# gMLP norm from batch-norm statistics, and a first norm by token halves

## The chip, the cores and the metric

The kernel runs on one core of a Trainium2 chip. The metric is the device time of the whole program in microseconds (us). TensorE is called PE, VectorE DVE, ScalarE ACT, GpSimd POOL and SyncE SP.

## The reference

256 tokens of width 1024 pass through two blocks of two layers each, all in fp32. The first block is, per layer, an RMS norm, a mixer (convolution and pooling in the even layer "ev", attention in the odd layer "od") and a gated feed-forward net. The second block has a latent-attention layer and a gMLP layer, each followed by a squared-ReLU net. What the change touches is the very first norm and the gMLP:

```python
def rmsnorm(x, g):
    y = xf * lax.rsqrt(jnp.mean(xf * xf, axis=-1, keepdims=True) + RMS_EPS)
    return (y * g).astype(x.dtype)

def even_mixer(h, w_in, conv_w, pool_w, pool_scale, w_out):
    z = h @ w_in                                  # 1024 -> 2048
    ...

def gmlp_mixer(h, w_in, ln_g, ln_b, ws, bs, w_out):
    z = jax.nn.gelu(h @ w_in, approximate=False)  # 1024 -> 4096
    u, v = z[..., :GM_HALF], z[..., GM_HALF:]     # GM_HALF = 2048
    v = layernorm(v, ln_g, ln_b)                  # mean and variance over 2048
    vc = v.reshape(B, S // GM_CHUNK, GM_CHUNK, GM_GROUPS, GM_GROUP_DIM)
    mixed = jnp.einsum('gpq,bnqgc->bnpgc', ws, vc) + bs.T[None, None, :, :, None]
    return (u * mixed.reshape(B, S, GM_HALF)) @ w_out
```

## The kernel before

**Weights.** All weights stream through four slots `raw` of 128 x 2048 numbers, loaded by SP in the order of use (`load(t)` for tile t, T_EV = 0 being the first). Every tile is split in two: ACT copies it to `w_hi` in PE's rounded fp32 (L508), DVE subtracts to get `w_lo` (L984), and each product is three matmuls (hi x hi, lo x hi, hi x lo). A slot of `raw` is loaded anew once DVE has split it (`lo_done`); `w_hi` and `w_lo` are written anew once PE has used the tile (`w_used`). `split(t)` is written into ACT's and DVE's programs by hand, and each engine works through its own program in order, so the place of a split among the other work decides when it runs.

**A norm.** Tokens lie on partitions, in two halves of 128 (`t` = 0, 1; the residual `h` is 128 x 2 x 1024). ACT squares and sums, POOL forms rstd, DVE scales (`hs`), PE transposes to features on partitions, ACT applies the gain (L533) and DVE makes `xn_hi` and `xn_lo` (`take`, L1010 and L1012). In most stages this goes by token halves (`norm` on ACT, `boundary` on DVE). The stage then begins with `head` on PE (L1717): the first two weight tiles are multiplied for token half 0 while half 1 is still in the norm (its transposes stand inside), then for half 1. The results have tokens on partitions; ACT copies them (`head_copy`, L574) and PE transposes them in the middle of the third tile (`head_out`, L1741).

**The first stage before.** x comes in one transfer, ahead of the first weight tile; then come sixteen transfers of small rows (gains, biases, convolution weights; L464) that PE transposes into `vec` (L1774), then the other weight tiles. The first norm runs over whole rows: `squares`, `scale`, `norm`, `gains`, `take`, in pieces of both halves. PE then does all eight input tiles with `f_tile` (L1609), 48 matmuls of 256 columns each, in banks 0 to 3, the first from L1622. The mixer's pooling and convolution on ACT and DVE run beside it. The pool matmuls are at L1791.

**gMLP.** PE first forms v in four column pieces c of 512, for both halves (`t_half`), two weight tiles a piece. ACT applies Gelu into `gm_v` with a sum beside it (L884). After the last piece DVE forms the mean (L1512, L1513), ACT squares the eight pieces less the mean (L894), DVE sums (L1516), POOL makes rstd (`root`, L2212 and L2214). DVE normalizes piece q with two operations for each half (`gm_norm`, L1528 and L1535) and copies a slice of 256 columns for PE (`gm_slice`, L1548). Meanwhile PE forms two tiles of u (`gm_u(0)`, `gm_u(1)`), and then mixes (`gm_mix`, L2159). A DVE step (`gm_step`, from L1554) adds the bias, multiplies by u and makes `a_lo` (L1566) for the output product; after the eighth step PE's `t_tail` (L1684) ends the stage. T_GM is the first u tile; T_GM + 2 and T_GM + 3 are the tiles that PE takes after the first mixing.

Of the kernel before, what the change touches and what calls it, by code (L numbers as in the profile page):

```python
# [23 lines left out]
ALU = mybir.AluOpType  # L24
# [3 lines left out]
P = 128  # L28
# [63 lines left out]
def build(nc, I, out):  # L92
    ctx = ExitStack()
    with ctx:
# [196 lines left out]
        in_h, in_cst, in_rows, in_small = sem("in_h"), sem("in_cst"), sem("in_rows"), sem("in_small")  # L291
# [46 lines left out]
        WHOLE = ("ev", "ctx")  # L338
# [159 lines left out]
        def _(act):  # L498
# [13 lines left out]
            def squares(name, src):  # L512

                for t in range(TT):
                    if name == "ctx":
                        act.wait_ge(ctx_in, 16)
                    else:
                        act.wait_ge(in_h, 16)
# [17 lines left out]
            def gains(name, gain, shift=None):  # L536
# [4 lines left out]
                if name == "ev":  # L541
                    act.wait_ge(vec_ready, 1)
# [1864 lines left out]
```

## Time and profile before

| | |
|---|---|
| median of three runs | 1346.9 us (1343.85 to 1347.37) |
| the profiled execution's own time | 1346.17 us |
| its span | 1344.4 us |
| PE busy | 1295.0 us, 96% |
| DVE busy | 940.4 us, 70% |
| ACT busy | 651.6 us, 48% |
| POOL busy | 117.0 us, 9% |
| DMA | 265.32 MB, mean 197 GB/s |
| mean granted PE clock | 0.983 |

The span is the profiled stretch on the core; the time around it is 1.8 us more. Busy shares are of the span. A matmul's duration in the trace runs to its modelled end, so matmuls that follow each other every 0.12 us are shown as 0.28 us each. Times in the rows are us from the span's start.

### The profile page before, as it was taken

How to read it: one execution, taken by the hardware profiler on the slowest of the kernel's cores; microseconds unless marked ns; L12 is line 12 of the kernel's file. 1: busy time of each engine (PE TensorE's matmuls, PEld its weight loads, DVE VectorE, ACT ScalarE, POOL GpSimd, SP SyncE). 2: the span in 40 equal slices, each digit the busy share in tenths (PEclk: the TensorE clock that was granted, in tenths of full speed). 3: DMA queues.
4: the chain of work that ended last, by engine and by line, in shares of the span. 5: the costliest groups of instructions: out<-in, count | busy, mean ns of one | idle time of the engine just before them, and what ended most of it. 6: DMA issues, size and time to landing. Idle time of an engine off the chain costs nothing.

```text
span 1344.4 us, 20759 instructions
## 1 busy us (share of the span) xinstructions
PE 1295.0 (96%) x8261; PEld 1155.8 (86%) x8261; DVE 940.4 (70%) x1168; ACT 651.6 (48%) x981; POOL 117.0 (9%) x226
## 2 busy tenths in 40 slices
PE   6999999999999999999789989999999899999998
PEld 5989999999777999999667768999888789889997
DVE  4867888856574688897455646998765589676654
ACT  4565444554353654454545635544445443554441
POOL 2000000000100021111012210111010000000000
PEclk9999999999998999999889999999999899999999
DMA  9636777745621498893222242999546378377540
GB/s 298 234 127 222 249 249 240 230 126 182 200 75 54 135 325 312 309 336 103 67 65 94 65 155 94 338 391 378 189 144 233 125 252 311 126 250 234 187 156 32
DMA packets 155660, 265.32 MB, mean 197 GB/s; under 512 B 5756, under 2 KB 116219, under 8 KB 155590
## 3 DMA queue, kind: packets, MB, share of 16 engines
q1 hardware_dynamic: 139094, 204.94, 45.6%
q0 software_dynamic: 16352, 58.98, 12.4%
q8 instruction: 49, 0.80, 0.2%
q10 hardware_dynamic: 144, 0.43, 0.1%
q14 instruction: 21, 0.17, 0.0%
HBM read 263.26 MB, written 1.06 MB: 197 GB/s over the span
## 4 chain that ended last, share of the span: by engine, by line
PE 85%; DVE 8%; ACT 3%; issue 2%; POOL 1%; DMA 0%; POOLq 0%; ACTq 0%; DVEq 0%
PE ps L1641 24%; PE ps L1622 12%; PE ps L1623 12%; PE ps L1624 12%; DVE w_lo L984 2%; PE ps L1684 2%; PE ps L1686 2%; PE ps L1685 2%; PE ps L1662 1%; PE ps L1664 1%; PE ps L1663 1%; PE ps L1733 1%; PE ps L1734 1%; PE ps L1735 1%; PE ps L2024 1%
## 5 line engine op out<-in xcount | busy, mean ns | idle before, releaser
L984 DVE TENSOR_TENSOR w_lo<-raw,w_hi 128x2048 fp32r<-128x2048 f32 (+3 forms) x215 | 442.7, 2071 | 137.9 <-ACT w_hi L508 137.6
L508 ACT ACTIVATE w_hi<-raw 128x2048 fp32r<-128x2048 f32 (+3 forms) x215 | 373.3, 1741 | 159.2 <-PE ps L1641 115.5
L1622 PE MATMUL ps<-xn_hi,w_hi 128*128 128x256 f32 x1440 | 411.3, 286 | 2.8 <-DVE xn_lo L1012 2.8
L1623 PE MATMUL ps<-xn_lo,w_hi 128*128 128x256 f32 x1440 | 409.5, 284 | 0.0
L1624 PE MATMUL ps<-xn_hi,w_lo 128*128 128x256 f32 x1440 | 409.3, 284 | 0.0
L1622 PEld LDWEIGHTS ps<-xn_hi,w_hi 128*128 128x128 f32 x1440 | 278.3, 193 | 5.6 <-issue 3.6
L1623 PEld LDWEIGHTS ps<-xn_lo,w_hi 128*128 128x128 f32 x1440 | 278.2, 193 | 2.2 <-issue 0.5
L1624 PEld LDWEIGHTS ps<-xn_hi,w_lo 128*128 128x128 f32 x1440 | 278.1, 193 | 0.0
L1641 PE MATMUL ps<-w_hi,a_hi 128*128 128x512 f32 x464 | 145.7, 395 | 0.9 <-DVE a_lo L1241 0.9
L1641 PE MATMUL ps<-w_lo,a_hi 128*128 128x512 f32 x464 | 144.1, 392 | 0.0
L1641 PE MATMUL ps<-w_hi,a_lo 128*128 128x512 f32 x464 | 143.6, 391 | 0.0
L1063 DVE SCALAR_TENSOR_TENSOR acc<-side,cs,acc 128x1024 f32<-128x1024 f32 x84 | 104.0, 1279 | 0.2
L1641 PEld LDWEIGHTS ps<-w_lo,a_hi 128*128 128x128 f32 x464 | 87.7, 189 | 19.0
L1641 PEld LDWEIGHTS ps<-w_hi,a_lo 128*128 128x128 f32 x464 | 87.4, 188 | 18.9
L1641 PEld LDWEIGHTS ps<-w_hi,a_hi 128*128 128x128 f32 x464 | 84.0, 190 | 16.5 <-DVE a_lo L1241 1.2
L2248 POOL DMA_DIRECT2D side<-in_ada_w x76 | 41.2, 542 | 355.6 <-DVE acc L1063 262.8
L853 ACT ACTIVATE work<-ps 128x512 f32<-128x512 f32 x32 | 19.1, 596 | 106.9 <-PE ps L1624 100.6
L647 ACT ACTIVATE work<-ps,vec 128x256 f32<-128x256 f32 x44 | 22.4, 560 | 85.8 <-PE ps L1624 79.4
L1178 DVE SCALAR_TENSOR_TENSOR work<-ps,vec,work 128x255 f32<-128x255 f32 (+1 forms) x88 | 38.3, 477 | 23.2 <-ACT work L647 21.0
L1684 PE MATMUL ps<-w_hi,a_hi 128*128 128x512 f32 x128 | 50.8, 397 | 0.7 <-DVE a_lo L1566 0.7
L1686 PE MATMUL ps<-w_hi,a_lo 128*128 128x512 f32 x128 | 49.9, 390 | 0.0
L1685 PE MATMUL ps<-w_lo,a_hi 128*128 128x512 f32 x128 | 49.9, 389 | 0.0
(293 smaller groups left out, 1795.4 us busy)
## 6 DMA issues: line engine op xcount, KB each, us to landing
raw<-in_ffn_w SPq DMA_DIRECT2D x64, 1024.0 KB, 5.6
side<-in_ada_w POOLq DMA_DIRECT2D x96, 512.0 KB, 6.4
raw<-in_ffn_w_in SPq DMA_DIRECT2D x44, 1024.0 KB, 5.4
raw<-in_ffn_w_out SPq DMA_DIRECT2D x32, 512.0 KB, 5.6
raw<-in_gm_w_in SPq DMA_DIRECT2D x16, 1024.0 KB, 5.8
raw<-in_od_w_in SPq DMA_DIRECT2D x12, 1024.0 KB, 5.5
raw<-in_ev_w_in SPq DMA_DIRECT2D x8, 1024.0 KB, 12.7
raw<-in_gm_w_out SPq DMA_DIRECT2D x8, 1024.0 KB, 5.6
```

The lines of the kernel that those rows point to most:

```text
L508: nc.scalar.activation(w_hi[s][:, 0:w], raw[s][:, 0:w], ACT.Copy).then_inc(hi_done, 1)
L984: nc.vector.tensor_tensor(w_lo[s][:, 0:w], raw[s][:, 0:w], w_hi[s][:, 0:w].bitcast(F32), ALU.subtract)\
L1063: nc.vector.scalar_tensor_tensor(acc[:, slot, :], tile, cs[:, bass.ds(val(kb), 1)], acc[:, slot, :], ALU.mult, ALU.add).then_inc(side_used, 1)
L1178: nc.vector.scalar_tensor_tensor(av, ps[bank][:, b * S:b * S + S - shift], vcol("ffn_conv_w", j * 2 + (n * 3 * FFB + tap * FFB + b)), av, ...
L1622: nc.tensor.matmul(o, hi, xn_hi3[:, k, :], start=k == 0, stop=False)
L1623: nc.tensor.matmul(o, hi, xn_lo3[:, k, :], start=False, stop=False)
L1624: last = nc.tensor.matmul(o, lo, xn_hi3[:, k, :], start=False, stop=k == KB - 1)
L1641: ins = nc.tensor.matmul(o, x_part, w, start=begin and x_part is xh and w_part == 0, stop=end and x_part is xl)
L1684: nc.tensor.matmul(o, xh, hi, start=first and i == 0 and m == 0, stop=False)
L1685: nc.tensor.matmul(o, xh, lo, start=False, stop=False)
L1686: last = nc.tensor.matmul(o, xl, hi, start=False, stop=i == 1 and m == len(blocks) - 1)
L2248: pool.dma_start(side[:, s.c % SLOTS, :], ada_view(layer, comp0 + m % n_comp, kb))\
```

## The change

**gMLP.** The Gelus give no sums any more. DVE takes batch-norm statistics (`bn_stats`, six numbers) of each piece of 512 for each half right behind its Gelu, and two `bn_aggr` merge the four sets of a half to mean and variance. POOL adds EPS to the variance and takes the power. ACT's eight squares and DVE's reductions are gone; ACT splits tiles T_GM + 2 and T_GM + 3 right behind the last Gelus. On DVE the splits of the two tiles stand behind the first norm and slice.

**The first stage.** x comes in two transfers with a semaphore each: half 0 first, then the sixteen small rows, then the first weight tile, then half 1, then the other tiles. The first norm goes by halves, and the stage uses `head`, `head_copy` and `head_out`. The banks of the six remaining tiles move by two.

```diff
@@ SP
-            sp.dma_start(h[:, :, :], I["x"][0].rearrange("(t p) d -> p t d", p=P)).then_inc(in_h, 16)
+            x_v = I["x"][0].rearrange("(t p) d -> p t d", p=P)
+            sp.dma_start(h[:, 0, :], x_v[:, 0, :]).then_inc(in_h[0], 16)
...
-            load(T_EV)
-
             at = 0
             stage = wk(6144, ROW_TILES * P).rearrange("p (r c) -> p r c", r=ROW_TILES)
             for name, n in ROWS:
...
+            load(T_EV)
+            sp.dma_start(h[:, 1, :], x_v[:, 1, :]).then_inc(in_h[1], 16)
             for t in range(T_EV + 1, T_FFN0):
                 load(t)
@@ ACT
-            squares("ev", h)
+            half_squares("ev", 0)
             split(T_EV)
-            gains("ev", lambda b: col("mix_norm_g", b))
+            half_gains("ev", 0, ev_gain)
+            half_squares("ev", 1)
             split(T_EV + 1)
+            half_gains("ev", 1, ev_gain)
+            head_copy("ev", T_EV)
             split(T_EV + 2)
             split(T_EV + 3)
...
+            act.wait_ge(head_ps, HEAD["ev"] + 1)
             for m in range(2):
-                act.wait_ge(w_used, T_EV + m + 1)
...
-                    nc.scalar.activation(gm_v[:, t, 512 * c:512 * c + 512], ps[GM_BANK[c] + t][:, :], ACT.Gelu,
-                                         accum_out=st[:, 48 + 4 * t + c:49 + 4 * t + c]).then_inc(GM["v"], 1)
-                if c < 3:
-                    split(T_GMV + 2 * c + 4)
-                    split(T_GMV + 2 * c + 5)
-            for t in range(TT):
-                act.wait_ge(GM["mu"], 1)
-                for c in range(4):
-
-                    junk = ps[4 + c][:, :] if t else acc[:, 3 + c // 2, 512 * (c % 2):512 * (c % 2) + 512]
-                    nc.scalar.activation(junk, gm_v[:, t, 512 * c:512 * c + 512], ACT.Square,
-                                         bias=st[:, 58 + t:59 + t], accum_out=st[:, 64 + 4 * t + c:65 + 4 * t + c])\
-                        .then_inc(GM["sq"], 1)
-            split(T_GM + 2)
-            split(T_GM + 3)
+                    nc.scalar.activation(gm_v[:, t, 512 * c:512 * c + 512], ps[GM_BANK[c] + t][:, :], ACT.Gelu).then_inc(GM["v"], 1)
+                split(T_GMV + 2 * c + 4)
+                split(T_GMV + 2 * c + 5)
@@ DVE
-            dve.wait_ge(in_h, 16)
-            scale("ev", h)
-            split(T_EV)
-
             dve.wait_ge(vec_ps, 1)
             nc.vector.tensor_copy(vec[:, 0:N_ROWS], ps[4][:, 0:N_ROWS]).then_inc(vec_ready, 1)
-            take("ev")
+            dve.wait_ge(in_h[0], 16)
+            half_scale("ev", 0)
+            split(T_EV)
+            take("ev", 0)
+            dve.wait_ge(in_h[1], 16)
+            half_scale("ev", 1)
...
             split(T_EV + 1)
+            take("ev", 1)
             split(T_EV + 2)
             split(T_EV + 3)
...
+            def gm_stats(c):
+                for t in range(TT):
+                    dve.wait_ge(GM["v"], 2 * c + t + 1)
+                    at = 40 + 24 * t + 6 * c
+                    nc.vector.bn_stats(st[:, at:at + 6], gm_v[:, t, 512 * c:512 * c + 512]).then_inc(GM["sq"], 1)
+
+            gm_stats(0)
...
+            for c in range(1, 3):
+                gm_stats(c)
+                split(T_GMV + 2 * c + 4)
+                split(T_GMV + 2 * c + 5)
+            gm_stats(3)
             dve.wait_ge(GM["sq"], 8)
-            nc.vector.tensor_reduce(st[:, 60:62], st[:, 64:72].rearrange("p (t c) -> p t c", t=TT), AX.X, ALU.add)\
-                .then_inc(GM["norm"], 1)
+            for t in range(TT):
+                nc.vector.bn_aggr(st[:, 4 + 2 * t:6 + 2 * t], st[:, 40 + 24 * t:64 + 24 * t]).then_inc(GM["norm"], 1)
...
-            split(T_GM + 2)
             gm_norm(0)
-            split(T_GM + 3)
...
             gm_slice(0)
+            split(T_GM + 2)
+            split(T_GM + 3)
@@ PE
             pe.wait_ge(in_cst, 16)
-            norm("ev")
...
             last.then_inc(vec_ps, 1)
+            transposes("ev", 0)
...
-            for m in range(8):
+            head("ev", T_EV)
+            for m in range(2, 8):
                 if m in free:
                     pe.wait_ge(*free[m])
-                f_tile(T_EV + m, m % 4, fresh="ev" if m == 0 else None)
+                else:
+                    pe.wait_ge(head_cp, 2 * HEAD["ev"] + m - 1)
+                f_tile(T_EV + m, (m - 2) % 4, mid=(lambda: head_out("ev")) if m == 2 else None)
@@ POOL
-            pool.wait_ge(GM["norm"], 1)
-            root(36, 2, [(60, 2, GMH)]).then_inc(GM["rstd"], 1)
+            pool.wait_ge(GM["norm"], 2)
+            for t in range(TT):
+                chain(nc.gpsimd.tensor_scalar(rs[:, 36 + t:37 + t], st[:, 5 + 2 * t:6 + 2 * t], 1.0, EPS, ALU.mult, ALU.add))
+            nc.gpsimd.tensor_tensor(rstd[:, 36:38], rs[:, 36:38], half[:, 0:2], ALU.pow).then_inc(GM["rstd"], 1)
```

The order of the work moves in two places. ACT at the start, before (L521 squares, L508 splits, L533 gains, L602 the first copy out of the input product):

```order
L521 ACTIVATE work,st<-h 128x1024 x2
L508 ACTIVATE w_hi<-raw 128x2048
L533 ACTIVATE work<-ps,vec 128x256 x8
L508 ACTIVATE w_hi<-raw 128x2048 x3
L590 ACT_TABLE_LOAD
```

and in the changed kernel (its own line numbers: L530 squares, L510 splits, L535 gains, L581 and L583 the two head copies), from half 1's squares on, with what each waits for (the same for half 0 and the first tile stands ahead of it):

```order
L530 ACTIVATE work,st<-h 128x512 [waits in_h1] x2
L510 ACTIVATE w_hi<-raw 128x2048 [waits raw_full1]
L535 ACTIVATE work<-ps,vec 128x128 [waits xt_ps,vec_ready]
L535 ACTIVATE work<-ps,vec 128x128 x3
L535 ACTIVATE work<-ps,vec 128x128 [waits xt_ps]
L535 ACTIVATE work<-ps,vec 128x128 x3
L581 ACTIVATE work<-ps 128x512 [waits head_t]
L583 ACTIVATE work<-ps 128x512 [waits w_used]
L510 ACTIVATE w_hi<-raw 128x2048 [waits raw_full2]
L510 ACTIVATE w_hi<-raw 128x2048 [waits raw_full3]
```

The splits of the third and fourth tile now stand behind the two head copies, the second of which waits until two tiles are used.

DVE around the gMLP norm, before (L984 splits, L1512 to L1516 sums, L1528 and L1535 the norm, L1548 the slice, L1554 the first step):

```order
L984 TENSOR_TENSOR w_lo<-raw,w_hi 128x2048 x4
L1512 TENSOR_REDUCE st<-st 128x2
L1513 TENSOR_SCALAR st<-st 128x2
L1516 TENSOR_REDUCE st<-st 128x2
L984 TENSOR_TENSOR w_lo<-raw,w_hi 128x2048
L1528 SCALAR_TENSOR_TENSOR work<-work,st,side 128x512 x2
L1535 SCALAR_TENSOR_TENSOR work<-work,rstd,side 128x512 x2
L984 TENSOR_TENSOR w_lo<-raw,w_hi 128x2048
L1548 COPY acc<-work 128x512
L1554 TENSOR_TENSOR acc<-ps,work 128x512
```

and in the changed kernel (L980 splits, L1534 and L1541 the norm, L1552 the slice, L1558 the first step):

```order
L1507 BN_STATS st<-work 128x6 x2
L980 TENSOR_TENSOR w_lo<-raw,w_hi 128x2048 x2
L1507 BN_STATS st<-work 128x6 x2
L1522 BN_AGGR st<-st 128x2 x2
L1534 SCALAR_TENSOR_TENSOR work<-work,st,side 128x512 x2
L1541 SCALAR_TENSOR_TENSOR work<-work,rstd,side 128x512 x2
L1552 COPY acc<-work 128x512
L980 TENSOR_TENSOR w_lo<-raw,w_hi 128x2048 x2
L1558 TENSOR_TENSOR acc<-ps,work 128x512
```

Both splits have moved behind the first slice, and the statistics stand behind each Gelu pair, ahead of the splits.

## Rows read from the trace of the kernel before

**Rows 1.** Who waited for whom, PE (total us, times, longest).

```profile
PE ps L2159 <- DVE acc L1548: 5.7, 1, 5.7
```

**Rows 2.** Timeline of PE's first real matmul; line L1791's matmuls (min/median/max ns).

```profile
17.46 0.35 PE L1622 MATMUL ps<-xn_hi,w_hi 128*128 128x256 f32 x1 [2.79 <-DVE xn_lo L1012]
...
L1791 PE MATMUL ps<-a_hi,w_hi x4: 283/283/283, 65.4 to 66.5; 128*128 128x256 f32 x4
```

**Rows 3.** Timeline of SP's issues: start us, us, what, [idle before].

```profile
1.88 1.99 SPq L464 DMA_DIRECT2D work<-in_mix_norm_g  x1
3.92 0.53 SPq L464 DMA_DIRECT2D work<-in_ffn_norm_g  x1
...
8.88 0.25 SPq L464 DMA_DIRECT2D work<-in_mla_k_norm  x1
...
9.53 25.90 SPq L409 DMA_DIRECT2D raw<-in_ev_w_in  x7
```

**Rows 4.** Timeline of ACT at the start.

```profile
10.36 1.91 ACT L508 ACTIVATE w_hi<-raw 128x2048 fp32r<-128x2048 f32 x1 [0.96 <-DMA raw<-in_ev_w_in]
15.29 3.03 ACT L533 ACTIVATE work<-ps,vec 128x256 f32<-128x256 f32 x8 [3.01 <-DVE vec L1103]
```

**Rows 5.** Timeline of ACT in gMLP, from the last Gelu to the tile splits.

```profile
1049.48 0.59 ACT L884 ACTIVATE work<-ps 128x512 f32<-128x512 f32 x1
...
1056.25 3.70 ACT L508 ACTIVATE w_hi<-raw 128x2048 fp32r<-128x2048 f32 x2
```

**Rows 6.** Timeline of POOL in gMLP.

```profile
1056.70 0.19 POOL L2212 TENSOR_SCALAR rs<-st 128x2 f32<-128x2 f32 x1 [43.77 <-DVE st L1516]
1056.97 0.72 POOL L2214 TENSOR_TENSOR rstd<-rs,half 128x2 f32<-128x2 f32 x1
```

**Rows 7.** Timeline of DVE in gMLP, from the mean to the first step.

```profile
1050.19 0.16 DVE L1512 TENSOR_REDUCE st<-st 128x2 f32<-128x8 f32 x1 [4.58 <-ACT work L884]
...
1058.25 2.29 DVE L984 TENSOR_TENSOR w_lo<-raw,w_hi 128x2048 fp32r<-128x2048 f32 x1 [1.64 <-ACT w_hi L508]
1060.46 1.41 DVE L1528 SCALAR_TENSOR_TENSOR work<-work,st,side 128x512 f32<-128x512 f32 x2
...
1065.56 0.42 DVE L1548 COPY acc<-work 128x512 f32<-128x512 f32 x1
1068.21 0.69 DVE L1554 TENSOR_TENSOR acc<-ps,work 128x512 f32<-128x512 f32 x1 [2.24 <-PE ps L2159]
```

**Rows 8.** Timeline of PE in gMLP: last of u, first and last mixing, tail.

```profile
1066.03 2.08 PE L2159 MATMUL ps<-work,acc 128*128 128x128 f32 x8 [5.67 <-DVE acc L1548]
...
1136.06 1.06 PE L2159 MATMUL ps<-work,acc 128*128 128x128 f32 x8
...
1144.63 0.47 PE L1684 MATMUL ps<-w_hi,a_hi 128*128 128x512 f32 x1 [0.66 <-DVE a_lo L1566]
```

**Rows 9.** Timelines of ACT (copy) and DVE (half norm) in the first stages.

```profile
34.14 0.58 ACT L602 ACTIVATE work<-ps 128x512 f32<-128x512 f32 x1
34.62 1.91 ACT L508 ACTIVATE w_hi<-raw 128x2048 fp32r<-128x2048 f32 x1
...
87.01 0.88 DVE L1000 TENSOR_SCALAR work<-h,rstd 128x512 f32<-128x512 f32 x2 [1.78 <-POOL rstd L2227]
...
89.72 0.29 DVE L1010 CAST xn_hi<-work 128x256 fp32r<-128x256 f32 x1 [1.23 <-ACT work L533]
...
90.39 0.28 DVE L1010 CAST xn_hi<-work 128x256 fp32r<-128x256 f32 x1
```

**Rows 10.** Page, DMA issues (KB, median us to landing); line L409's landing, window 9.5:10.

```profile
raw<-in_ev_w_out SPq DMA_DIRECT2D x4, 1024.0 KB, 5.0
...
DMA to landing us min/median/max: 5.9/5.9/5.9
```

**Rows 11.** PE by stretches: us, busy (x), granted clock, DMA share, GB/s.

```profile
18.40:21.85 3.45, 3.42 (x17) 0.53 0.78 183
1066.00:1069.80 3.80, 3.77 (x17) 0.50 0.82 233
```

More of the change, by code:

```diff
@@ L290, in build @@
         side_used = sem("side_used")
-        in_h, in_cst, in_rows, in_small = sem("in_h"), sem("in_cst"), sem("in_rows"), sem("in_small")
+        in_h = [sem(f"in_h{t}") for t in range(TT)]
+        in_cst, in_rows, in_small = sem("in_cst"), sem("in_rows"), sem("in_small")
         vec_ps, vec_ready, cs_ready = sem("vec_ps"), sem("vec_ready"), sem("cs_ready")
@@ L336, in build @@
         RCOL = dict({n: 2 * k for n, k in NORM.items()}, final=18)
-        WHOLE = ("ev", "ctx")
+        WHOLE = ("ctx",)
         def counts(names, whole, halves):
@@ L350, in build @@
         XN = counts(NORM, 4, 8)
-        HEAD = {n: k for k, n in enumerate(["ffn0", "od", "ffn1", "relu0", "relu1"])}
-        TB = {"ffn0": (2, 3), "od": (2, 3), "ffn1": (2, 3), "lat": (2, 4), "relu0": (4, 5), "gm": (2, 3), "relu1": (2, 3)}
+        HEAD = {n: k for k, n in enumerate(["ev", "ffn0", "od", "ffn1", "relu0", "relu1"])}
+        TB = {"ev": (2, 3), "ffn0": (2, 3), "od": (2, 3), "ffn1": (2, 3), "lat": (2, 4), "relu0": (4, 5), "gm": (2, 3), "relu1": (2, 3)}
         def u_at(j, base):
@@ L514, in squares @@
                 for t in range(TT):
[L515 to L518, printed above, removed]
+                    act.wait_ge(ctx_in, 16)
                     c = RCOL[name] + t
-                    junk = wk(4096 + D * t, D) if name == "ctx" else hs[:, t, :]
+                    junk = wk(4096 + D * t, D)
                     nc.scalar.activation(junk, src[:, t, :], ACT.Square, accum_out=st[:, c:c + 1]).then_inc(sq_done, 1)
@@ L526, in half_squares @@
                 for c in range(2):
-                    act.wait_ge(h_ready, h_count(name, t, c))
+                    if name == "ev":
+                        act.wait_ge(in_h[t], 16)
+                    else:
+                        act.wait_ge(h_ready, h_count(name, t, c))
                     nc.scalar.activation(hs[:, t, 512 * c:512 * c + 512], h[:, t, 512 * c:512 * c + 512], ACT.Square,
@@ L554, in half_gains @@
                     act.wait_ge(mod_ready, MOD_COUNT[name])
+                if name == "ev":
+                    act.wait_ge(vec_ready, 1)
                 for i in range(4):
@@ L597, in _ @@
             ev_u = wk(2564, 4 * 272).rearrange("p (g t) -> p g t", g=4)
+            act.wait_ge(head_ps, HEAD["ev"] + 1)
             for m in range(2):
-                act.wait_ge(w_used, T_EV + m + 1)
                 if m == 0:
                     act.wait_ge(EV["pin"], 1)
-                nc.scalar.activation(ev_u[:, 2 * m:2 * m + 2, 16:272], ps[m][:, :].rearrange("p (g t) -> p g t", g=2), ACT.Copy)\
+                nc.scalar.activation(ev_u[:, 2 * m:2 * m + 2, 16:272], ps[2 + m][:, :].rearrange("p (g t) -> p g t", g=2), ACT.Copy)\
                     .then_inc(EV["pool"], 1)
@@ L607, in _ @@
                 act.wait_ge(w_used, t + 1)
-                nc.scalar.activation(ev_c, ps[(2 + 3 * m) % 4][:, :], ACT.Copy).then_inc(EV["gate"], 1)
+                nc.scalar.activation(ev_c, ps[3 * m % 4][:, :], ACT.Copy).then_inc(EV["gate"], 1)
                 split(t + 4)
@@ L1160, in _ @@
             dve.wait_ge(rows_ps, 1)
-            nc.vector.tensor_copy(bias_rows, ps[2][0:8, 0:511]).then_inc(rows_sb, 1)
+            nc.vector.tensor_copy(bias_rows, ps[0][0:8, 0:511]).then_inc(rows_sb, 1)
             for j in range(2):
@@ L1507, in _ @@
                 nc.vector.tensor_copy(gm_wst[:, 512 * c:512 * c + 512], ps[6 + c][:, :]).then_inc(GM["ws"], 1)
-            for j in range(2, 6):
-                split(T_GMV + j + 4)
-            dve.wait_ge(GM["v"], 8)
-            chain(nc.vector.tensor_reduce(st[:, 56:58], st[:, 48:56].rearrange("p (t c) -> p t c", t=TT), AX.X, ALU.add))
-            nc.vector.tensor_scalar(st[:, 58:60], st[:, 56:58], -1.0 / GMH, None, ALU.mult).then_inc(GM["mu"], 1)
-            dve.wait_ge(GM["mu"], 1)
+            for c in range(1, 3):
[3 more added lines that the diff above has]
+            gm_stats(3)
             dve.wait_ge(GM["sq"], 8)
-            nc.vector.tensor_reduce(st[:, 60:62], st[:, 64:72].rearrange("p (t c) -> p t c", t=TT), AX.X, ALU.add)\
-                .then_inc(GM["norm"], 1)
+            for t in range(TT):
+                nc.vector.bn_aggr(st[:, 4 + 2 * t:6 + 2 * t], st[:, 40 + 24 * t:64 + 24 * t]).then_inc(GM["norm"], 1)
+            dve.wait_ge(GM["norm"], 2)
             dve.wait_ge(GM["rstd"], 1)
@@ L1527, in gm_norm @@
                 for t in range(TT):
-                    last = nc.vector.scalar_tensor_tensor(vv[t], vv[t], st[:, 58 + t:59 + t], gain, ALU.add, ALU.mult)
+                    last = nc.vector.scalar_tensor_tensor(vv[t], vv[t], st[:, 4 + 2 * t:5 + 2 * t], gain, ALU.subtract, ALU.mult)
                 if q % 2:
@@ L1788, in _ @@
             for g in range(4):
-                o = ps[g // 2][:, (g % 2) * S:(g % 2) * S + S]
+                o = ps[2 + g // 2][:, (g % 2) * S:(g % 2) * S + S]
                 hi, lo = parts(T_POOL % SLOTS, g * P, P)
@@ L1802, in _ @@
                     pe.wait_ge(rb_ready, 16)
-                    nc.tensor.matmul(ps[2][0:8, 0:511], rel[:, :], onehot, start=True, stop=True).then_inc(rows_ps, 1)
+                    nc.tensor.matmul(ps[0][0:8, 0:511], rel[:, :], onehot, start=True, stop=True).then_inc(rows_ps, 1)
             def ev_ready(i):
```

11 lines of the change are left out of this document (6 added, 5 removed).

## The prediction

> **What bounds the kernel now.** I first read who waited for whom on TensorE (PE). PE is busy for 96% of the span, so an edit counts only where PE stands still or where PE gets more to do. Two of its waits lie where the change works: 5.7 us for the first slice of the gMLP norm (L1548) [rows 1], and the start, where the first real matmul waits for `xn_lo` (L1012). From 17.46 us to the pool matmuls at 65.4 us PE doesn't stop again [rows 2].
>
> The start: the SP queue issues all of x and the first weight tile, then sixteen row transfers from 1.88 us, and the other tiles from 9.53 us [rows 3]. The first tile can be split by ScalarE (ACT) at 10.36 us, and the eight gain copies run from 15.29 us [rows 4].
>
> The gMLP norm: between the last Gelu and the first mixing matmul there is a chain. ACT ends the Gelu at 1050.1 us, squares eight pieces, and only then splits the next two weight tiles, from 1056.25 us [rows 5]. GpSimd gives rstd at 1057.7 us [rows 6]. VectorE (DVE) waits for the tile split, not for rstd: split (2.29), norm from 1060.46 us, a second split, slice at 1065.56 us [rows 7]. PE ends its second u tile at 1060.4 us and mixes at 1066.03 us, at half clock [rows 8].
>
> **Part 1, the gMLP norm.** The eight squares, their eight reads, two reductions and the eight reads behind the Gelus go; eight bn_stats and two bn_aggr come on DVE. Six bn_stats stand in stretches where DVE waits for ACT (4.58 us idle before L1512 [rows 7]; the same kind of gap is there behind each Gelu pair), so they cost nothing; only the last pair is on the chain. No row shows a bn_stats. From below it is half of the 0.88 us of two tensor-scalars over 512 [rows 9], 0.44 us; from above two passes at 1.41/2 = 0.7 us each [rows 7], 1.4 us. I take one such pass, 0.7 us, as the row that reads as many fp32 numbers once. An aggregate over 24 numbers I put at 0.2 us.
>
> The new chain: the last Gelu ends at 1050.1; its bn_stats 0.7, two aggregates 0.4; GpSimd now two small operations (0.27 from start to start, by 1056.70 and 1056.97 [rows 6]) and the power 0.72, so 1.3; hand-overs 0.2. DVE starts its norm at 1052.7. Norm 2.9 (the 5.1 from 1060.46 to the slice at 1065.56, less 2.2 for the split that now goes behind), slice 0.4: done at 1056.0, 4.4 us before PE is through with the u tiles. So PE's wait of 5.7 us goes wholly. The two splits (4.5 us) follow, DVE is free at 1060.5. ACT makes its halves of them from 1050.1 to 1053.8, in the place of the squares.
>
> What is late next: the mixing matmuls start at 1060.4, and at full clock eight take 1.06 us instead of 2.08 [rows 8]. DVE's first step therefore starts at 1061.4, not at 1068.21 [rows 7]: **6.8 us** earlier. From that step on DVE is the tighter engine: its steps follow each other with only the 0.7 and 1.1 us for ACT's half between them, down to the last `a_lo`, for which PE waits at 1144.63 [rows 8]. So what PE wins beyond 6.8 us, by running its next u tile at full clock as well, it loses there, where its wait grows from 0.66 to some 1.5 us. Gain: 6.8 us; if bn_stats costs 1.4 us, DVE is free at 1062.0 and the gain is 6.2.
>
> **Part 2, the start.** The first weight tile now stands behind x's first half and the sixteen row transfers. The fifteen later rows are issued from 3.92 to 9.53 us [rows 3]; the first took 1.99 us with 2 MB in flight ahead of it, which I put at 0.5 when only half of x is. The rows start at 1.4 (the 1.88 of before less the weight tile's own issue), so the weight tile is issued at 1.4 + 0.5 + 5.6 = 7.5, and a little less if the others speed up too: I take 7.3. Bounds: 7.0 and 9.5. A 1 MB tile takes 5.0 us to landing on a quiet queue and took 5.9 at 9.53 us [rows 10]; I take 5.2. It lands at **L = 12.5**, against 10.36 at the latest before. The Trainium skill, DMA: Bandwidth & Descriptors, section Anatomy of one DMA, gives 2.0 us plus the bytes at 436 GB/s, an estimate of 4.4 us for 1 MB: by it L would be 11.7 and the sum 0.8 us smaller. By that formula the trace does not agree: 5.0 and 5.9 us [rows 10].
>
> From L on, each with its row [rows 4, 7, 9, 11]: ACT half 1.9, DVE half 2.3, first cast and rest 0.7, hand-overs 0.3. The first matmul starts at L + 5.2 = 17.7, so hardly later than now (17.46): the landing is later by 2 us, but gains and rows are no longer behind it. Then:
> - Second tile: DVE first takes half 0 (four times 0.67), scales half 1 (0.9) and splits (2.3): ready at L + 10.3 = 22.8. The 24 matmuls on the first tile's first half are done at 20.6, or 22.8 at half clock. PE goes on at 22.9.
> - 24 matmuls at 0.12 us (384 of them fill 17.46 to 65.4 us less 1.7 for the clock [rows 2, 11]), 2.9; half 1's eight transposes, now inside, 0.9; token half 1's 48 matmuls 5.8, 0.2 for their first operand: the head ends at L + 20.1 = 32.6.
> - **The new wait.** ACT's queue now has the two head copies ahead of the split of the third tile, and the second copy waits until both tiles are used up. In the norms further on, both splits stand ahead of the copies. So PE finishes the head and then stands still for a copy (0.5 until ACT's next start [rows 9]), the ACT half 1.9, the DVE half 2.3, hand-overs 0.2: **4.9 us**. The third tile starts at 37.5.
> - Six tiles at 5.76 us, 34.6, and the eight head transposes, 0.9. After the 2.79 us of idling at the start PE ran 3.4 us at a granted clock of 0.53, and after 5.67 us of idling in gMLP 3.8 us at 0.50 (1.2 of 2.4 GHz) [rows 11]: half of each stretch, 1.6 and 1.9 us, was lost. I take 1.7 here.
>
> The pool matmuls start at 74.6 instead of 65.4: **+9.2 us**. What follows is the old order with its banks renamed, and PE-bound; the side loads of GpSimd go out some 6 us later, are wanted only in the first feed-forward stage, and cost nothing. The second half of x lands right behind the first tile, before its squares are due. Bounds: a rows pace of before without any relief and a landing of 5.9 us make L 15.4 and the term 12.1, rows issued by 7.0 and 5.0 us to landing (L = 12.0) and a clock that costs 0.7 make it 7.7.
>
> **Sum.** +9.2 - 6.8 = +2.4 us. The profiled execution took 1346.17 us (span 1344.4), 0.7 under the median of 1346.9, so the sum gives 1348.6 on its own scale and 1349.3 on the median's. A measurement of this kernel tells some 0.3%, 4.0 us, from no change; +2.4 is within.
>
> **The rivals.**
> - *The start costs more, slower by over 0.3%.* Mechanism: the row transfers keep their pace of before and hold the first weight tile back in SP's queue; each us of L is a us of the end. It decides from L = 14.1 on (+10.8 - 6.8). For it: one row still took 0.25 us to issue late in the series [rows 3]; against it: the 1.99 us of the first one went with 2 MB in flight. At L = 15.4: +5.3, 1352.2. A clock that stays low for twice as long (+1.7) does the same from L = 12.4. Chance 0.28.
> - *The wait behind the head is hidden.* If PE were held at the third tile less than I think, for example because the clock stays up, the term is 7.7 and the sum +0.9 or, with PE's whole gain in gMLP (7.6, if DVE weren't the tighter one), +0.1: 1347.0 to 1347.8, still no difference. Inside my 0.64.
> - *Faster by over 0.3%.* The change of order would have to cost under 2.8 us. It does if the third tile's split is not on the path, which the order of ACT's queue speaks against: without the 4.9 us and the 1.7 of clock the sum is -4.2, 1342.7. Chance 0.08.
> - *bn_stats is dear, over 3 us a piece.* Then the last pair pushes the norm out by 4.8 us, DVE is free at 1065.3, and the gain falls to 2.9: 1353.2. Every one-pass row over 512 numbers says no; 0.03, within the slower case.
>
> **How the numbers follow.** Within 0.3%: 0.64, my forecast, +2.4 us with its own range of -1 to +4. Slower 0.28, faster 0.08. The range must leave out 2 in 10: 1345.8 takes in the small start term (+0.9) and 2 us for a median of three runs that spread over 3.5 us; 1353.0 takes in the late landing of the first tile.
>
> **What would show each step.** The first real matmul near 17.7 us, PE's second wait near 22 us, a third wait of 4.9 us ahead of the third tile with ACT's queue on a copy, a low granted clock behind it, the pool matmuls near 74.6 us. In gMLP no wait at the first mixing matmul and no low clock there; bn_stats near 0.7 us; the distance from the last Gelu to the last `a_lo` shorter by 6.8 us; PE's wait before it near 1.5 us. I am wrong if the third tile starts right behind the head, if the first tile lands after 14 us, or if another stage moves.

## The result, and the profile after

Over 17 runs of each on the same chip, the kernel before took 1346.05 us (1338.64 to 1347.37) and the changed one 1349.95 us (1345.95 to 1353.39). The ratio is 1.0029, with a 95% interval of 1.0017 to 1.0042: 3.9 us slower, the size of what a measurement of this kernel can just tell from nothing. The forecast was 1349.3 us, 2.4 us slower.

| | before | after |
|---|---|---|
| profiled execution's own time | 1346.17 us | 1353.39 us |
| its span | 1344.4 us | 1351.7 us |
| PE busy | 1295.0 us | 1300.1 us |
| DVE busy | 940.4 us | 946.5 us |
| ACT busy | 651.6 us | 647.3 us |
| mean granted PE clock | 0.983 | 0.982 |

The profiled execution is the longest of the 17, so part of its 7.3 us of extra span has to be found in something that other executions don't show.

I read first who waited for whom on PE. The columns are, as in [rows 1], total us, times and longest:

```profile
PE ps L1778 <- DMA work<-in_ada_b: 8.8, 1, 8.8
PE ps L1739 <- DVE xn_lo L1008: 6.3, 3, 5.8
...
PE ps L1628 <- DVE w_lo L980: 4.9, 1, 4.9
...
PE ps L1690 <- DVE a_lo L1570: 1.1, 1, 1.1
```

The wait of 5.7 us for the first slice [rows 1] is gone, and a new one of 4.9 us stands there, for the split of a weight tile. The last row is the end of gMLP, where PE waited 0.66 us before [rows 8]. PE's timeline at the start, those rows that begin after idling, shows where:

```profile
18.44 0.55 PE L1739 MATMUL ps<-w_hi,xn_hi 128*128 128x256 f32 x1 [5.77 <-DVE xn_lo L1008]
38.60 0.55 PE L1628 MATMUL ps<-xn_hi,w_hi 128*128 128x256 f32 x1 [4.90 <-DVE w_lo L980]
```

The first real matmul is 1 us later than in [rows 2]. There is no wait ahead of the second tile in this trace: PE went through the first tile's matmuls at half pace until 23.70 us, and the second tile's split was done at 23.3. The third tile starts at 38.60 us, and the pool matmuls, last row below, 11.2 us later than in [rows 2]:

```profile
L1799 PE MATMUL ps<-a_hi,w_hi x4: 283/283/283, 76.6 to 77.7; 128*128 128x256 f32 x4
```

The timeline of SP (against [rows 3]) shows how the first tile comes to be late:

```profile
1.31 0.41 SPq L464 DMA_DIRECT2D work<-in_mix_norm_g  x1
1.78 0.41 SPq L464 DMA_DIRECT2D work<-in_ffn_norm_g  x1
...
7.36 0.43 SPq L411 DMA_DIRECT2D raw<-in_ev_w_in  x1
```

The first row now goes out in 0.41 us instead of 1.99, the others take as long as before, and the tile is issued at 7.36 us. The answer for this one issue gives its landing:

```profile
DMA to landing us min/median/max: 6.0/6.0/6.0
```

ACT's timeline (against [rows 4]) shows both the late tile and the order of the queue:

```profile
13.39 1.91 ACT L510 ACTIVATE w_hi<-raw 128x2048 fp32r<-128x2048 f32 x1 [6.28 <-DMA raw<-in_ev_w_in]
...
28.23 0.65 ACT L581 ACTIVATE work<-ps 128x512 f32<-128x512 f32 x1
33.74 0.60 ACT L583 ACTIVATE work<-ps 128x512 f32<-128x512 f32 x1 [4.86 <-PE ps L1741]
34.23 3.70 ACT L510 ACTIVATE w_hi<-raw 128x2048 fp32r<-128x2048 f32 x2
```

From 28.88 to 33.74 us ACT stands at the second head copy until PE has used both tiles; the splits of the third and fourth tile are queued behind it. PE, through with the head, then waits for the copy, ACT's half (1.9) and DVE's half of the third tile. That is the wait of 4.90 us. What it costs afterwards is in PE's stretches (us, PE, PEld, DVE, ACT and POOL busy with counts, granted clock, DMA share, GB/s):

```profile
38.40:44.20 5.80, 5.60 (x26) 5.63 (x27) 2.26 (x2) 1.05 (x2) 0.00 (x0) 0.50 0.79 252
...
790.10:809.40 19.30, 17.37 (x49) 10.47 (x49) 5.64 (x9) 2.43 (x6) 0.00 (x0) 0.73 0.22 76
```

Behind the wait PE runs at half clock (1.2 of 2.4 GHz) until 44.2 us: of 5.6 us, 2.8 are lost. The second row is a stretch some 750 us later, in a stage that the change doesn't edit. It ran at a mean granted clock of 0.73 and took 19.3 us; the execution profiled of before has the same 49 matmuls at full clock in 14.6 us:

```profile
780.70:795.30 14.60, 12.61 (x49) 8.04 (x50) 5.64 (x9) 2.44 (x7) 0.00 (x0) 1.00 0.30 101
```

gMLP after, DVE's timeline (against [rows 7]):

```profile
1063.66 1.29 DVE L1507 BATCH_NORM_STATS2 st<-work 128x6 f32<-128x512 f32 x2 [4.10 <-ACT work L892]
1064.98 0.39 DVE L1522 BATCH_NORM_AGGREGATE st<-st 128x2 f32<-128x24 f32 x2
1066.82 1.42 DVE L1534 SCALAR_TENSOR_TENSOR work<-work,st,side 128x512 f32<-128x512 f32 x2 [1.44 <-issue]
...
1069.72 0.43 DVE L1552 COPY acc<-work 128x512 f32<-128x512 f32 x1
1070.06 4.49 DVE L980 TENSOR_TENSOR w_lo<-raw,w_hi 128x2048 fp32r<-128x2048 f32 x2
1075.51 0.69 DVE L1558 TENSOR_TENSOR acc<-ps,work 128x512 f32<-128x512 f32 x1 [0.96 <-PE ps L2167]
```

The statistics of two pieces take 1.29 us and the two aggregates 0.39. The slice is done at 1070.15 us, and PE, which needs it next, takes it without a wait and at full clock, and so against [rows 8] in 1.06 us, not 2.08:

```profile
1074.35 1.06 PE L2167 MATMUL ps<-work,acc 128*128 128x128 f32 x8
```

**Where the 7.3 us of span are.** I took DVE's 215 tile splits of both traces in pairs and read how far each starts behind its counterpart, which gives the lag at every point of the program. It is +11.0 us once the first stage is under way, 14.15 us ahead of the gMLP norm, and +7.3 us from the first split behind it to the end. So: start +11.2 us, gMLP -6.85 us, and +2.95 us from other places: +4.8 us in the stretch at a clock of 0.73, less what other stretches gave back. Is that stretch the change's doing? Read from 775 to 812 us, the traces of this case show a granted clock of 0.86 here, of 0.95 in two more kernels with the new first stage, and of 1.00 in the other two with it and in all four with the old one, though PE idles for the same 1.88 us there in all nine. With one execution of each kernel that does not tell chance from an effect of the later start; it stays open. The medians, over 17 runs each, are 3.9 us apart, about what the start's and gMLP's parts come to without that stretch.

### The profile page after: what moved, and what is told of

The parts are those of the page before. It is cut to its first block, busy times and chain, and to the rows that moved or that the text cites. A ratio compares the mean times of both kernels' runs of the same rounds, so it can differ in the third digit from the quotient of the medians.

```text
span 1351.7 us, 20790 instructions
## 1 busy us (share of the span) xinstructions
PE 1300.1 (96%) x8269; PEld 1158.7 (86%) x8269; DVE 946.5 (70%) x1185; ACT 647.3 (48%) x971; POOL 117.3 (9%) x229
## 3 DMA queue, kind: packets, MB, share of 16 engines
HBM read 263.26 MB, written 1.06 MB: 196 GB/s over the span
## 4 chain that ended last, share of the span: by engine, by line
PE 86%; DVE 8%; ACT 3%; issue 2%; POOL 1%; DMA 0%; SPq 0%; POOLq 0%; ACTq 0%; DVEq 0%
PE ps L1647 24%; PE ps L1628 12%; PE ps L1630 12%; PE ps L1629 12%; DVE w_lo L980 2%; PE ps L1739 2%; PE ps L1690 2%; PE ps L1692 2%; PE ps L1691 2%; PE ps L1668 1%; PE ps L1741 1%; PE ps L1740 1%; PE ps L1669 1%; PE ps L1670 1%; PE ps L2032 1%
## 5 line engine op out<-in xcount | busy, mean ns | idle before, releaser
L980 DVE TENSOR_TENSOR w_lo<-raw,w_hi 128x2048 fp32r<-128x2048 f32 (+3 forms) x215 | 442.7, 2072 | 132.7 <-ACT w_hi L510 132.4
L510 ACT ACTIVATE w_hi<-raw 128x2048 fp32r<-128x2048 f32 (+3 forms) x215 | 373.1, 1741 | 155.5 <-PE ps L1647 116.0
L1628 PE MATMUL ps<-xn_hi,w_hi 128*128 128x256 f32 x1408 | 402.5, 286 | 4.9 <-DVE w_lo L980 4.9
L1630 PE MATMUL ps<-xn_hi,w_lo 128*128 128x256 f32 x1408 | 400.7, 285 | 0.0
L1629 PE MATMUL ps<-xn_lo,w_hi 128*128 128x256 f32 x1408 | 400.7, 285 | 0.0
L1628 PEld LDWEIGHTS ps<-xn_hi,w_hi 128*128 128x128 f32 x1408 | 272.5, 194 | 7.3 <-issue 5.6
L1647 PE MATMUL ps<-w_hi,a_hi 128*128 128x512 f32 x464 | 146.7, 398 | 1.1 <-DVE a_lo L1239 0.9
L1647 PE MATMUL ps<-w_lo,a_hi 128*128 128x512 f32 x464 | 144.8, 393 | 0.0
L1647 PE MATMUL ps<-w_hi,a_lo 128*128 128x512 f32 x464 | 144.4, 392 | 0.0
L1739 PE MATMUL ps<-w_hi,xn_hi 128*128 128x256 f32 x192 | 56.9, 296 | 6.4 <-DVE xn_lo L1008 6.3
L1740 PE MATMUL ps<-w_lo,xn_hi 128*128 128x256 f32 x192 | 55.3, 288 | 0.0
L1741 PE MATMUL ps<-w_hi,xn_lo 128*128 128x256 f32 x192 | 55.3, 288 | 0.0
```

The lines of the kernel that those rows point to most:

```text
L510: nc.scalar.activation(w_hi[s][:, 0:w], raw[s][:, 0:w], ACT.Copy).then_inc(hi_done, 1)
L980: nc.vector.tensor_tensor(w_lo[s][:, 0:w], raw[s][:, 0:w], w_hi[s][:, 0:w].bitcast(F32), ALU.subtract)\
L1628: nc.tensor.matmul(o, hi, xn_hi3[:, k, :], start=k == 0, stop=False)
L1629: nc.tensor.matmul(o, hi, xn_lo3[:, k, :], start=False, stop=False)
L1630: last = nc.tensor.matmul(o, lo, xn_hi3[:, k, :], start=False, stop=k == KB - 1)
L1647: ins = nc.tensor.matmul(o, x_part, w, start=begin and x_part is xh and w_part == 0, stop=end and x_part is xl)
```

## The experiments

Each kernel ran in five rounds beside the kernel before; ratios are against it, with 95% intervals. Four ran on one chip (before: 1344.29 us, 26 runs), the last three on another (1344.58 us, 27 runs). The first two kernels run the two halves of the sum apart, the next two ask what the start loses by, two more what in gMLP gives the gain, and the last repairs the start.

### gMLP's part alone

The kernel before, with only the gMLP part of the change:

```diff
-                    nc.scalar.activation(gm_v[:, t, 512 * c:512 * c + 512], ps[GM_BANK[c] + t][:, :], ACT.Gelu,
-                                         accum_out=st[:, 48 + 4 * t + c:49 + 4 * t + c]).then_inc(GM["v"], 1)
+                    nc.scalar.activation(gm_v[:, t, 512 * c:512 * c + 512], ps[GM_BANK[c] + t][:, :], ACT.Gelu).then_inc(GM["v"], 1)
...
+            gm_stats(3)
...
-            split(T_GM + 2)
             gm_norm(0)
-            split(T_GM + 3)
...
             gm_slice(0)
+            split(T_GM + 2)
+            split(T_GM + 3)
```

> The kernel before with the gMLP part of the change alone. My theory: the two parts add up, so this one gives -6.8 us (ratio 0.995), all of it between the last Gelu and DVE's first gMLP step; the first stage is as before. Rival: the gMLP part gains nothing by itself, because DVE's work behind it is as tight as before (ratio 1.000).

Measured: 1337.17 us (1331.73 to 1340.04, 9 runs), ratio 0.9952 (0.9935 to 0.997), 6.5 us faster. DVE's timeline is the one of the changed kernel, 17 us earlier:

```profile
1046.55 1.29 DVE L1497 BATCH_NORM_STATS2 st<-work 128x6 f32<-128x512 f32 x2 [4.09 <-ACT work L884]
...
1058.40 0.69 DVE L1548 TENSOR_TENSOR acc<-ps,work 128x512 f32<-128x512 f32 x1 [0.97 <-PE ps L2155]
```

From the start of the statistics to the first step it is 11.85 us in both. The lag of the splits falls by 6.8 us over the norm. So this part is worth what the prediction gave it, and it works without the other one.

### The start's part alone

The kernel before, with only the first stage's part of the change (x in two transfers, the first tile behind the rows, the norm by halves, the head).

```diff
+            load(T_EV)
+            sp.dma_start(h[:, 1, :], x_v[:, 1, :]).then_inc(in_h[1], 16)
...
+            half_gains("ev", 1, ev_gain)
+            head_copy("ev", T_EV)
             split(T_EV + 2)
             split(T_EV + 3)
```

> The kernel before with the first-stage part of the change alone. My theory: +10.7 us (ratio 1.008): a first matmul 1 us later, 1.7 us more of PE work inside, 4.9 us of waiting for the third tile, and some 3 us at half clock behind that wait. Rival: the start costs no more than 4 us, and the rest of the loss seen lies elsewhere (ratio 1.003).

Measured: 1354.69 us (1353.12 to 1359.88, 6 runs), ratio 1.0094 (1.0077 to 1.0111): 12.6 us slower by the ratio, 10.4 us between the medians, from six runs that spread over 6.8 us. PE's timeline, rows after idling:

```profile
18.09 0.55 PE L1743 MATMUL ps<-w_hi,xn_hi 128*128 128x256 f32 x1 [5.34 <-DVE xn_lo L1020]
...
37.98 0.55 PE L1632 MATMUL ps<-xn_hi,w_hi 128*128 128x256 f32 x1 [4.90 <-DVE w_lo L992]
```

The same 4.90 us again. Its half clock lasts less here:

```profile
37.90:42.10 4.20, 4.12 (x19) 4.15 (x20) 2.13 (x1) 0.92 (x2) 0.00 (x0) 0.50 0.68 218
```

and the pool matmuls start at 75.3 us, 9.9 us later than in [rows 2]. So the trace and the medians stand by the 10.7 us expected; the ratio's interval, 10.3 to 14.9 us, holds it too. Together with the first experiment: -0.48% and +0.94% make +0.46%, with some 0.25% of uncertainty; the whole change measured +0.29%. The two parts add up as far as these runs can tell.

### The two splits ahead of the head copies

The changed kernel with the two splits and the head copies in the other order on ACT:

```diff
             half_gains("ev", 1, ev_gain)
-            head_copy("ev", T_EV)
             split(T_EV + 2)
             split(T_EV + 3)
+            head_copy("ev", T_EV)
```

> The changed kernel, with ACT's splits of the third and fourth tile ahead of the two head copies. My theory: PE goes from the head straight into the third tile, so 4.9 us of waiting and up to 2.9 us of half clock go: -5 to -8 us against the changed kernel, 1342 to 1345 us, below the kernel before. Rival: the third tile is late for another reason (its transfer, or DVE's half), and less than 2 us goes.

Measured: 1341.48 us (1337.29 to 1344.46, 11 runs), ratio 0.9978 (0.9965 to 0.9991). Against the changed kernel's 1.0029 that is 0.51% less, 6.9 us, with some 0.18% (2.4 us) of uncertainty. ACT's timeline:

```profile
27.57 3.77 ACT L510 ACTIVATE w_hi<-raw 128x2048 fp32r<-128x2048 f32 x2
31.18 0.65 ACT L581 ACTIVATE work<-ps 128x512 f32<-128x512 f32 x1
33.09 0.60 ACT L583 ACTIVATE work<-ps 128x512 f32<-128x512 f32 x1 [1.26 <-PE ps L1741]
```

PE doesn't wait at the third tile any more, and there is no half clock behind it:

```profile
28.00:34.00 6.00, 6.00 (x53) 6.00 (x52) 5.36 (x5) 4.72 (x5) 0.00 (x0) 1.00 1.04 399
34.00:44.00 10.00, 10.00 (x87) 10.00 (x86) 4.72 (x4) 8.18 (x8) 0.00 (x0) 1.00 0.87 277
```

The pool matmuls start at 68.3 us instead of 76.6, and 2.9 us behind the kernel before. So most of what the start loses is this one wait and the clock that falls in it, not the late first tile.

### The first tile ahead of the rows

```diff
+            load(T_EV)
             at = 0
...
-            load(T_EV)
             sp.dma_start(h[:, 1, :], x_v[:, 1, :]).then_inc(in_h[1], 16)
```

> The changed kernel, with the first weight tile issued ahead of the sixteen row transfers, behind x's first half; ACT's order is as in the change. My theory: the tile lands near 9 us instead of 13.4, the path then goes over the rows and DVE's scale and split, the first matmul starts near 15.7 instead of 18.4 and the second tile is ready near 20.8 instead of 23.3: -2.6 us against the changed kernel; the wait ahead of the third tile stays at 4.9 us. Rival: the rows then land so late that nothing is won (0 us).

Measured: 1345.37 us (1340.98 to 1349.75, 11 runs), ratio 1.0013 (0.9999 to 1.0027); 0.16% less than the change, with 0.19% of uncertainty, so not told from it. Here the trace tells more than the time. The tile lands 4.3 us earlier (ACT splits it from 9.10 us instead of 13.39), but PE's timeline is only this much ahead:

```profile
11.64 0.86 PE L1778 MATMUL ps<-cst,work 128*128 128x128 f32 x3 [11.64 <-DMA work<-in_ada_b]
...
16.88 0.55 PE L1739 MATMUL ps<-w_hi,xn_hi 128*128 128x256 f32 x1 [1.38 <-DVE xn_lo L1008]
22.45 0.39 PE L1739 MATMUL ps<-w_hi,xn_hi 128*128 128x256 f32 x1 [1.14 <-DVE w_lo L980]
37.41 0.55 PE L1628 MATMUL ps<-xn_hi,w_hi 128*128 128x256 f32 x1 [4.90 <-DVE w_lo L980]
```

The rows, which now come behind the tile, land 2.8 us later (11.64 against 8.8 us), and both the transposes of half 0 and the gains stand behind them in the queues of PE and ACT. The third tile is 1.2 us earlier (37.41 against 38.60), not the 2.6 expected: a miss. What the late tile costs, the late rows cost as well.

### The statistics, with DVE's splits in their old places

The kernel before with the new statistics (as in the first experiment), but on DVE `split(T_GM + 2)` ahead of `gm_norm(0)` and `split(T_GM + 3)` behind it, as before:

```diff
+            gm_stats(3)
...
             split(T_GM + 2)
             gm_norm(0)
             split(T_GM + 3)
```

> The kernel before with the statistics of the change, but DVE's two splits stay where they were (one ahead of the first norm, one between norm and slice). My theory: with rstd ready 5 us earlier, DVE comes to its slice at 1059.9 and is free for the first step by 1060, so PE doesn't wait either way: -6.8 us against the kernel before, as with the whole gMLP part (ratio 0.995). Rival: the gain is that of the moved splits, and without them half or more of it is lost (ratio 0.998 or more).

Measured: 1337.7 us (1331.9 to 1340.62, 10 runs), ratio 0.994 (0.9916 to 0.9965). The lag of the splits falls by 6.5 us over the norm, where it falls by 6.8 with the splits moved. DVE's timeline:

```profile
1049.14 0.39 DVE L1512 BATCH_NORM_AGGREGATE st<-st 128x2 f32<-128x24 f32 x2
1050.97 2.29 DVE L972 TENSOR_TENSOR w_lo<-raw,w_hi 128x2048 fp32r<-128x2048 f32 x1 [1.45 <-POOL rstd L2323]
...
1058.28 0.42 DVE L1544 COPY acc<-work 128x512 f32<-128x512 f32 x1
1060.02 0.69 DVE L1550 TENSOR_TENSOR acc<-ps,work 128x512 f32<-128x512 f32 x1 [1.32 <-PE ps L2155]
```

With both splits back in the chain, the slice is still in time. The statistics alone bring the gain; moving DVE's splits adds 0.3 us in the traces and nothing that the times can tell.

### The splits behind the slice, with the old sums

The kernel before with that half of the gMLP part alone:

```diff
-            split(T_GM + 2)
             gm_norm(0)
-            split(T_GM + 3)
...
             gm_slice(0)
+            split(T_GM + 2)
+            split(T_GM + 3)
```

> The kernel before with its squares, but DVE's two splits moved behind the first slice. My theory: rstd is there at 1057.7 as before, the slice is done near 1061.1, PE's wait of 5.7 us shrinks to 0.8; but DVE still has both splits to do and starts its first step near 1065.6 instead of 1068.2, so the time falls by 2.6 us only (ratio 0.998), and the rest comes up as a wait of PE further on in gMLP. Rival: PE's wait is what counts, and 5 us go with it (ratio 0.996).

Measured: 1343.32 us (1338.58 to 1344.6, 12 runs), ratio 0.9987 (0.9966 to 1.0007): not told from no change, with the span 2.2 us shorter in the trace. PE's timeline at the first mixing, with two of its waits, and from the list of who waited for whom a third:

```profile
1061.74 1.16 PE L2159 MATMUL ps<-work,acc 128*128 128x128 f32 x8 [0.74 <-DVE acc L1546]
...
1064.03 0.36 PE L1622 MATMUL ps<-xn_hi,w_hi 128*128 128x256 f32 x1 [1.14 <-DVE w_lo L984]
...
PE ps L1641 <- DVE a_lo L1564: 1.3, 2, 0.8
```

PE's wait of 5.67 us at the mixing [rows 8] falls to 0.74, and the time by no more than 2.2 us in the trace. The wait at the mixing goes, but DVE has to make the splits in any case, and they stand in its queue ahead of the first step, which starts at 1066.0 instead of 1068.21 us [rows 7]. This execution came to the stage 0.6 us late, so 2.8 us were gained in it; 2.6 had been expected. The rest came back as waits: 1.14 us for the next split, 1.3 for `a_lo` where the kernel before has none, and 1.1 instead of 0.66 us at the last `a_lo`. This is the clearest place to see that the stage's second half is bound by DVE: 4.9 us less waiting at the mixing, and only 2.2 us less to the first step.

### The start repaired

The changed kernel with the first tile early, the splits ahead of the head copies, and the rows off the path: half 0 is scaled and transposed ahead of the rows' transposes, and half 1's squares stand ahead of half 0's gains.

```diff
@@ SP
+            load(T_EV)
             at = 0
...
-            load(T_EV)
@@ ACT
             split(T_EV)
-            half_gains("ev", 0, ev_gain)
             half_squares("ev", 1)
+            half_gains("ev", 0, ev_gain)
             split(T_EV + 1)
             half_gains("ev", 1, ev_gain)
-            head_copy("ev", T_EV)
             split(T_EV + 2)
             split(T_EV + 3)
+            head_copy("ev", T_EV)
@@ DVE
-            dve.wait_ge(vec_ps, 1)
-            nc.vector.tensor_copy(vec[:, 0:N_ROWS], ps[4][:, 0:N_ROWS]).then_inc(vec_ready, 1)
             dve.wait_ge(in_h[0], 16)
             half_scale("ev", 0)
             split(T_EV)
+            dve.wait_ge(vec_ps, 1)
+            nc.vector.tensor_copy(vec[:, 0:N_ROWS], ps[4][:, 0:N_ROWS]).then_inc(vec_ready, 1)
@@ PE
+            transposes("ev", 0)
             pe.wait_ge(in_rows, 16 * N_ROW_DMAS)
...
             last.then_inc(vec_ps, 1)
-            transposes("ev", 0)
```

> The changed kernel with the first tile ahead of the rows, with both splits ahead of the head copies, and with half 0's scale and transposes ahead of the rows' transposes and copy (ACT squares half 1 ahead of half 0's gains). My theory: with the tile early the rows became the gate (the trace of that run has PE waiting for them until 11.64 us); now the first matmul starts near 15.3 us instead of 16.9, the third tile near 30.5 instead of 37.4, without a wait: 2 us less than with the splits first alone, ratio 0.996 against the kernel before. Rival: DVE's half of the second tile, not the rows, is the gate; then the first matmul comes earlier and the third tile does not (33 us).

Measured: 1338.21 us (1336.5 to 1340.09, 12 runs), ratio 0.9954 (0.9935 to 0.9972). PE's timeline:

```profile
8.95 1.94 PE L1720 MATMUL ps<-cst,work 128*128 128x128 f32 x8 [8.95 <-DVE work L996]
11.56 0.89 PE L1779 MATMUL ps<-cst,work 128*128 128x128 f32 x3 [0.67 <-DMA work<-in_ada_b]
15.45 0.55 PE L1739 MATMUL ps<-w_hi,xn_hi 128*128 128x256 f32 x1 [3.01 <-DVE xn_lo L1008]
20.37 0.38 PE L1739 MATMUL ps<-w_hi,xn_hi 128*128 128x256 f32 x1 [0.17 <-DVE w_lo L980]
...
30.28 0.28 PE L1628 MATMUL ps<-xn_hi,w_hi 128*128 128x256 f32 x1
```

The last row is the third tile: it starts at 30.28 us, where 30.5 had been expected and 33 by the rival, and without a wait. The first real matmul is 2 us earlier than in [rows 2], yet the pool matmuls start at 65.7 us, where they started before (65.4). From the first real matmul to the pool matmuls it is 50.3 us here and 47.9 in the kernel before. The 2.3 us between them go mainly to the head's own costs, which the whole-row norm doesn't have: the eight transposes of half 1 and the eight of its output, that PE now makes inside the tiles (taken as 1.8 us in the prediction; the time at half pace at the start is about the same in both, 17 and 18 matmuls). The time equals that of gMLP's part alone (0.9952). Both are faster than the kernel before and than the changed one by more than their intervals; between the two of them, and the one with DVE's splits in their old places (0.994), the runs don't tell.

## Why the prediction held, and where its terms were off

- **gMLP, -6.8 us.** Measured at -6.85 in the trace, and alone at -6.8 in its trace and -6.5 by the times. bn_stats taken at 0.7 us was 0.645 (1.29/2), an aggregate at 0.2 was 0.195, GpSimd's three operations 1.27 us (taken as 1.3). The slice was done 4.2 us ahead of PE; the prediction said 4.4. From the end of the last Gelu (1064.1 us now) to the first step it is 11.4 us, by the prediction's times (1050.1 to 1061.4) 11.3. PE's wait ahead of the last `a_lo` grew from 0.66 [rows 8] to 1.1 us, not to 1.5. The rival in which bn_stats costs over 3 us is out by a factor of nearly five. The Trainium skill, VectorE: DVE Perf Modes, section on the TRN2 errata, has a formula for an fp32 add of two tensors that gives 691 ns for 512 elements; this trace agrees (0.69 us at L1558, an add that reads one of its two tensors from `ps`), and bn_stats lies just below it.
- **The landing L, 12.5 us.** It was 13.4 (13.0 in the trace with the splits first). The issue was right (7.3 said, 7.36 measured): only the first row went faster. The term that was mis-sized is the transfer, taken as the 5.0 us of a quiet queue and a little more: 6.0 us. That x's second half and further tiles, issued right behind it (from 7.83 us on), made it so is argued from the 5.9 of [rows 10], which stood in the same situation; no run varies it. The estimate of 4.4 us from the Trainium skill, DMA: Bandwidth & Descriptors, section Anatomy of one DMA, is still further from the trace. That section gives its formula for transfers issued by GpSimd, and this one was issued by SP. It made 0.9 us of the end.
- **The wait behind the head, 4.9 us.** It was 4.90 us in all three kernels that have this order, whatever else was varied. That it is caused by ACT's queue is shown by the experiment that moves the splits: wait gone, 6.9 us less. The rival by which the wait is hidden is out with this row, and so is the faster one, whose only ground was that the third tile's split might not be on the path.
- **The clock behind it, 1.7 us.** The size varies, for one and the same wait of 4.90 us: half clock for 5.6 us in the changed kernel's trace, 4.1 us with the start alone, 2.9 us with the early tile, so 2.8, 2.0 and 1.5 us lost. 1.7 lay among them; the profiled execution had the longest, which is 1.1 of its +11.2 against +9.2. The reference moves too: in the four traces that have the old start, the pool matmuls begin at 64.8, 65.4, 65.7 and 65.8 us, and 13, 18, 22 and 23 of the matmuls at its beginning go at half pace, 0.21 us apart.
- **The sum, +2.4 us.** The medians say +3.9, with an interval of 2.3 to 5.7 us. The start's term is 9.9 to 11.2 us in the traces, where 9.2 was said; in the changed kernel's trace 0.9 of the 2.0 between them is the landing and 1.1 the clock behind the wait. The head took 10.0 us from its second tile to its end, where 9.7 was said; the wait ahead of the second tile, looked for near 22 us, is not in this trace, and is 0.2 to 0.3 us at 23.0 in those of the start alone and of the splits first. The two terms of the sum at their measured sizes (9.9 to 11.2, less 6.8) give +3.1 to +4.4 us, so the median is not met by errors that cancel. The forecast and its 64% for a difference within 0.3% stand, at their edge: 0.29%. The slower rival's mechanism, rows that keep their pace and hold the tile back, was half there: all rows but the first kept it, and the tile came 0.9 us later than forecast, short of the 14.1 us from which it would have decided.
- **What was expected wrongly on the way.** The experiment with the early tile took the first tile for the start's only gate. With the tile early the rows are the later ones (11.64 us against the tile's 9.10), and the prediction's chain from L on ("gains and rows are no longer behind it") was true only as long as the tile was the last to land.

Left open: how much of the half clock behind the wait an average run has, since only one execution of each kernel has a trace; what made the stretch near 800 us slow; and why the early tile's order brings 1.2 us at the third tile rather than the 1.6 of the first matmul (18.44 against 16.88). The rows show the second tile 1.1 us late there, at a split that ACT began at 17.99 us, behind the gains and half 1's squares; that this is the reason is argued, not tried by itself.

## What to carry to other kernels

When a stage is cut into halves, look at each engine's queue for the step that waits for the consumer (here a copy that waits until PE has used two tiles) and put the preparation of the next tiles ahead of it: here another place for one call was worth 6.9 us of the some 10 that the start had lost. A wait that goes on the busiest engine is worth only what the next engine's queue lets through; read the first step behind it, not the wait. And gains and losses of one change that stand in different stages should be run apart: here a sum near zero held a part worth 6.5 us that could be had alone.

## What the runs showed of the hardware

- Batch-norm statistics of 128 x 512 fp32 numbers took DVE 0.645 us, less than the 0.71 us of one two-tensor operation of that size (1.42/2), and replaced one ACT square, its read of the sum, the Gelu's read of its sum and a share of two reductions.
- The same idle time of 4.90 us on PE was followed by 2.9, 4.1 and 5.6 us at half clock in three executions.
- At the very start the recorded clock and the matmuls disagree. In the changed kernel's trace a stretch is recorded at full clock,

```profile
18.40:23.70 5.30, 5.26 (x25) 5.29 (x25) 4.80 (x11) 1.98 (x3) 4.89 (x9) 1.00 1.10 349
```

and yet its matmuls follow each other every 0.21 us, 25 in 5.3 us, and only from 23.70 us on every 0.12 us:

```profile
23.48 0.41 PE L1741 MATMUL ps<-w_hi,xn_lo 128*128 128x256 f32 x1
23.70 0.31 PE L1739 MATMUL ps<-w_hi,xn_hi 128*128 128x256 f32 x1
23.85 0.28 PE L1740 MATMUL ps<-w_lo,xn_hi 128*128 128x256 f32 x1
```

That is the pace of the lower level: behind the wait, where 0.50 is recorded, 26 of them take 5.6 us. The Trainium skill, TensorE: Matmul & The Clock Gate, section Seeing it yourself, warns that recorded clock events have been unreliable on trn2; here the spacing had to be read in their place.
- Issuing a small row took SP 0.25 to 0.57 us, the 0.57 for the first one behind 1.5 MB issued in two transfers (the early tile). Behind 2 MB in two transfers the first one took 1.99 us. What makes the difference no run shows.
